# Values as weights in two attentions, X split beside a gate product, and query blocks in groups of two

## Chip, cores and metric

One core of a Trainium2 chip runs the whole program. The metric is the device time of one execution in microseconds (us). TensorE (PE) multiplies, VectorE (DVE) and ScalarE (ACT) work on its results, GpSimd (POOL) prepares weights, SyncE (SP) issues loads.

## What is computed

Three layers on 512 tokens of width 1024, in float32. The parts that matter here:

```python
def forgetting_attention(q, k, v, log_f):      # first layer, 8 heads of 64
    sc = q @ k.T * scale + (c[t] - c[s]),  causal
    return softmax(sc) @ v                     # then * silu(fg)
...
# second layer ends with
x = x + sigmoid(x @ ple_w_gate + ple_b_gate) * (p @ ple_w_proj)
...
def swa_sink_attention(x, pos, k_sh, v_sh, w_q, b_q, sinks, w_o, b_o):   # third layer, 16 query heads, 4 key heads
    scores = q @ kb * A_HEAD_DIM ** -0.5       # a block of 128 queries sees its own and the block before: 256 keys
    m = maximum(max(scores), sink); e = exp(scores - m)
    probs = e / (sum(e) + exp(sink - m))
    return (probs @ vb) @ w_o + b_o            # k_sh, v_sh = split(x @ kv_w + kv_b)
```

## The kernel before, in words

X lies with features on the partitions and the 512 tokens along the free dimension (8 tiles of 128x512). Every large product splits both factors into a high and a low part (fp32r) and sums three products per tile in a PSUM bank: high x high, high x low weights, low x high (lines 575 to 577). The weights stream in 238 blocks of 128x1024 through `W_raw`, and POOL splits them into `W_hi` and `W_lo`. Each engine has its own program, written by hand in the order in which it runs; semaphores join them. A table (`PHASES`, `PLAN`) lists the products, which engine reads their banks, and so which count a later tile waits for before it takes one of the four accumulation banks (`bank_free`). Some products are woven (`weave`): their first three tiles run together, feature tile by feature tile, while A is still being made.

The first attention (`softmax_attention(FOX, ...)`) has four pairs of heads and, for each, four query blocks (steps) with 128, 256, 384 and 512 keys. A step on TensorE: scores of both heads (each head in one half of the rows of the array), gates and mask added by bf16 products, transposes of the probabilities, and the weighing, where the transposed probabilities `PT` are the stationary operand and 64 columns of values move (line 772). A float32 matmul is two records in the trace, a transpose one. The output of a pair has tokens on the partitions, is scaled by the inverse sums (VectorE, line 1649), and turned back by four transposes (`turn_outputs`, line 719). The second attention (SWA) has eight pairs, four steps each, with 128 keys in the first and 256 in the others; both heads of a step go through one maximum (line 1616), four or two exponents on ACT (line 1183), transposes, a copy and the weighing. Two sets of score banks alternate by step (`score_bank`). The product of its values (`v3`) gives features on the partitions, and is turned by eight transposes.

In `embed(0)` ACT takes the sigmoid of each gate tile into `GATE`, VectorE multiplies by the projection and adds to X; when ACT has taken all eight, it splits X into `A_hi`, which the gate product itself still reads until then, and VectorE makes `A_lo` for the rotary product `rope3`, which is woven.

```python
                sums(f"gate{l}", into(lambda i: GATE[:, i, :], ACT.Sigmoid, f"ple_b{l}"))
                for i in range(KD):
                    if l == 0:
                        split(X[:, i, :], i, "ple0", embedded, i + 1)
```

## Time and profile before

| | us |
|---|---|
| median of three runs | 1557.76 (1557.06 to 1558.67) |
| the profiled execution | 1559.97 |
| its span, first to last instruction | 1556.9 |
| TensorE busy | 1529.2 |
| POOL, VectorE, ACT busy | 902.4, 715.6, 419.9 |

The span is what the trace shows; the profiled execution's own time includes 3.1 us outside it. TensorE's granted clock is full in every slice of the page. A busy TensorE is not TensorE at its peak, since records of matmuls overlap: the pace is read from start to start.

### The profile page before, as it was taken

How to read it: one execution, taken by the hardware profiler on the slowest of the kernel's cores; microseconds unless marked ns; L12 is line 12 of the kernel's file. 1: busy time of each engine (PE TensorE's matmuls, PEld its weight loads, DVE VectorE, ACT ScalarE, POOL GpSimd, SP SyncE). 2: the span in 40 equal slices, each digit the busy share in tenths (PEclk: the TensorE clock that was granted, in tenths of full speed). 3: DMA queues.
4: the chain of work that ended last, by engine and by line, in shares of the span. 5: the costliest groups of instructions: out<-in, count | busy, mean ns of one | idle time of the engine just before them, and what ended most of it. 6: DMA issues, size and time to landing. Idle time of an engine off the chain costs nothing.

```text
span 1556.9 us, 19863 instructions
## 1 busy us (share of the span) xinstructions
PE 1529.2 (98%) x7220; PEld 1239.3 (80%) x7220; DVE 715.6 (46%) x877; ACT 419.9 (27%) x845; POOL 902.4 (58%) x719
## 2 busy tenths in 40 slices
PE   9999999999999999999999999999999999999998
PEld 7777777788888788888888877867878888888876
DVE  5674566350026576103531255667667400552255
ACT  3223545133113332001210044655142200221031
POOL 7656023676631778666766655800549766776644
PEclk9999999999999999999999999999999999999999
DMA  6223011323320323333333322300213332222322
GB/s 208 95 82 95 15 41 35 101 81 95 95 68 20 114 75 115 95 95 95 94 99 104 95 68 81 122 15 1 83 53 122 100 102 95 95 95 95 98 78 81
DMA packets 36837, 132.30 MB, mean 85 GB/s; under 512 B 4105, under 2 KB 4385, under 8 KB 36770
## 3 DMA queue, kind: packets, MB, share of 16 engines
q1 hardware_dynamic: 35282, 128.16, 26.3%
q10 hardware_dynamic: 1488, 3.17, 0.6%
q8 instruction: 51, 0.84, 0.2%
q14 instruction: 16, 0.13, 0.0%
HBM read 129.20 MB, written 2.10 MB: 84 GB/s over the span
## 4 chain that ended last, share of the span: by engine, by line
PE 90%; DVE 4%; ACT 4%; DMA 1%; issue 1%; ACTq 0%; SPq 0%; DVEq 0%
PE PS L575 22%; PE PS L577 22%; PE PS L576 22%; PE PS L548 2%; PE PS L772 2%; PE PS L543 2%; PE PS L544 2%; PE PS L757 1%; PE PS L732 1%; PE PS L929 1%; DVE A_lo L1488 1%; PE PS L600 1%; PE PS L601 1%; PE PS L602 1%; PE PS L692 1%; PE PS L690 1%
## 5 line engine op out<-in xcount | busy, mean ns | idle before, releaser
L501 POOL TENSOR_TENSOR W_lo<-W_raw,W_hi 128x1024 fp32r<-128x1024 f32 x238 | 600.9, 2525 | 19.8
L498 POOL TENSOR_TENSOR HOLD<-HOLD 1x1 f32<-1x1 f32 x238 | 62.9, 264 | 616.4 <-PE PS L577 342.1
L575 PE MATMUL PS<-A_hi,W_hi 128*128 128x512 f32 x984 | 385.0, 391 | 0.0
L577 PE MATMUL PS<-A_lo,W_hi 128*128 128x512 f32 x984 | 382.9, 389 | 0.0
L576 PE MATMUL PS<-A_hi,W_lo 128*128 128x512 f32 x984 | 382.8, 389 | 0.0
L499 POOL TENSOR_SCALAR W_hi<-W_raw 128x1024 fp32r<-128x1024 f32 x238 | 247.2, 1039 | 0.0
L575 PEld LDWEIGHTS PS<-A_hi,W_hi 128*128 128x128 f32 x984 | 184.7, 188 | 39.7 <-issue 1.1
L576 PEld LDWEIGHTS PS<-A_hi,W_lo 128*128 128x128 f32 x984 | 184.7, 188 | 39.1 <-issue 1.0
L577 PEld LDWEIGHTS PS<-A_lo,W_hi 128*128 128x128 f32 x984 | 184.7, 188 | 38.7
L575 PE MATMUL PS<-H_hi,W_hi 128*128 128x512 f32 x512 | 199.2, 389 | 0.0
L576 PE MATMUL PS<-H_hi,W_lo 128*128 128x512 f32 x512 | 199.2, 389 | 0.0
L577 PE MATMUL PS<-H_lo,W_hi 128*128 128x512 f32 x512 | 199.2, 389 | 0.0
L1843 DVE TENSOR_TENSOR H_lo<-SQR,H_hi 128x512 f32 (+1 forms) x64 | 122.6, 1915 | 57.4 <-ACT H_hi L1383 57.4
L1380 ACT ACTIVATE RELU<-PS 128x512 f32<-128x512 f32 x64 | 38.0, 594 | 308.5 <-PE PS L577 300.7
L1841 DVE TENSOR_TENSOR SQR<-RELU 128x512 f32<-128x512 f32 x64 | 81.3, 1270 | 79.9 <-ACT RELU L1380 79.9
L576 PEld LDWEIGHTS PS<-H_hi,W_lo 128*128 128x128 f32 x512 | 96.1, 188 | 20.1
L577 PEld LDWEIGHTS PS<-H_lo,W_hi 128*128 128x128 f32 x512 | 96.1, 188 | 20.0
L575 PEld LDWEIGHTS PS<-H_hi,W_hi 128*128 128x128 f32 x512 | 96.1, 188 | 19.7
L1790 DVE TENSOR_TENSOR X<-X,PS 128x512 f32<-128x512 f32 x32 | 21.9, 687 | 177.9 <-PE PS L577 177.9
L1787 DVE SCALAR_TENSOR_TENSOR X<-X,PS 128x512 f32<-128x512 f32 x24 | 16.4, 687 | 173.4 <-PE PS L577 167.7
L1348 ACT ACTIVATE SQ<-X 128x512 f32<-128x512 f32 x28 | 17.8, 636 | 198.5 <-DVE X L1790 176.2
L543 PE MATMUL PS<-A_hi,W_hi 128*128 128x512 f32 x168 | 66.4, 396 | 2.1 <-ACT A_hi L1066 2.1
(293 smaller groups left out, 1978.6 us busy)
## 6 DMA issues: line engine op xcount, KB each, us to landing
W_raw<-in_weights SPq DMA_DIRECT2D x238, 512.0 KB, 3.5
X<-in_x SPq DMA_DIRECT2D x4, 512.0 KB, 6.3
out<-X ACTq DMA_DIRECT2D x8, 256.0 KB, 2.8
RELU<-in_ple_in ACTq DMA_DIRECT2D x2, 512.0 KB, 3.5
CONST<-in_constants SPq DMA_DIRECT2D x1, 849.5 KB, 10.1
PARAM<-in_params SPq DMA_DIRECT2D x1, 197.5 KB, 3.7
CONST<-in_constants SPq DMA_DIRECT2D x1, 192.0 KB, 8.6
NEG_C<-FF_PART ACTq DMA_DIRECT2D x3, 8.0 KB
```

What stands on the lines that cost most here:

```text
L498: pool.tensor_tensor(HOLD[:, 1 + s:2 + s], HOLD[:, 0:1], HOLD[:, 0:1], ALU.add)
L499: pool.tensor_scalar(W_hi[:, s, :], W_raw[:, r, :], 1.0, 1.0, ALU.mult, ALU.mult).then_inc(w_hi, 1)
L501: pool.tensor_tensor(W_lo[:, s, :], W_raw[:, r, :], W_hi[:, s, :].bitcast(F32), ALU.subtract).then_inc(w_lo, 1)
L543: pe.matmul(PS[:, i, :], W_hi[:, slot, w], hi[:, k, :], start=k == 0, stop=False)
L544: pe.matmul(PS[:, i, :], W_lo[:, slot, w], hi[:, k, :], start=False, stop=False)
L548: done = pe.matmul(PS[:, i, :], W_hi[:, slot, w], lo[:, k, :], start=False, stop=k == KD - 1)
L575: pe.matmul(PS[:, bank, :], W_hi[:, slot, w], hi[:, kk, :], start=first, stop=False)
L576: pe.matmul(PS[:, bank, :], W_lo[:, slot, w], hi[:, kk, :], start=False, stop=False)
L577: done = pe.matmul(PS[:, bank, :], W_hi[:, slot, w], lo[:, kk, :], start=False, stop=last)
L1380: act.activation(RELU[:, slot, :], bank, ACT.Relu).then_inc(by_act, 1)
L1841: dve.tensor_tensor(SQR[:, slot, :], RELU[:, slot, :], RELU[:, slot, :], ALU.mult).then_inc(h_sq, 1)
L1843: dve.tensor_tensor(H_lo[:, i, :], SQR[:, slot, :], H_hi[:, i, :].bitcast(F32), ALU.subtract).then_inc(h_lo, 1)
```

## The change

Both attentions now keep the values stationary: 64 columns of values per head are the weights and 128 columns of transposed probabilities move, one head into the upper, the other into the lower half of the output's partitions. The output so has features on the partitions, no transposes follow, and the inverse sums are spread over partitions by eight small products per pair (`spread_inverse`); VectorE multiplies the bank by them (`SHARE`). The second attention goes by groups of two query blocks: the two blocks of both heads share two score banks, with the mask put in first, and one maximum covers both blocks (1024 elements). Its values product has tokens stationary and 256 columns of weights moving, so the values need no turning, and the bias is now 256 columns of parameters. The first scores are issued ahead of that product, the second behind it. X after the gate product goes into buffers of its own (`B_hi`, `B_lo`): ACT splits tile i - 3 right behind the sigmoid of tile i, the gate is worked out in its PSUM bank, and the bank is freed by VectorE's addition instead of ACT.

```diff
-        ("down{0}b", 8, 2, "dve"), ("proj{0}b", 4, 0.25, "act"), ("gate{0}", 8, 1, "act")]
+        ("down{0}b", 8, 2, "dve"), ("proj{0}b", 4, 0.25, "act"), ("gate{0}", 8, 1, "dve")]
...
-PHASES += [("rope3", 10, 1, "act"), ("v3", 2, 1, "act"), ("out3", 8, 1, "dve")]
+PHASES += [("rope3", 10, 1, "act"), ("v3", 2, 1, "dve"), ("out3", 8, 1, "dve")]
...
-                ("head_g", 8), ("b_rope", 10), ("b_v", 2), ("sinks", Q_HEADS), ("b_o", 8),
+                ("head_g", 8), ("b_rope", 10), ("sinks", Q_HEADS), ("b_o", 8),
                 ("mix_g0", 8), ("mix_b0", 8), ("mlp_g0", 8), ("mlp_b0", 8), ("ple_b0", 8),
-                ("mix_g1", 8), ("mix_b1", 8), ("mlp_g1", 8), ("mlp_b1", 8), ("ple_b1", 8), ("w_pool", 2 * P)]
+                ("mix_g1", 8), ("mix_b1", 8), ("mlp_g1", 8), ("mlp_b1", 8), ("ple_b1", 8), ("w_pool", 2 * P), ("b_v", 2 * P)]
...
+            def window_values():
+
+                ph, banks = PLAN["v3"], VALUE_BANKS["v3"]
+
+                def multiply(b, t, k):
+                    slot, tokens = (ph.first + b) % W_SLOTS, slice(t * P, t * P + P)
+                    w = slice(k % 4 * 2 * P, (k % 4 + 1) * 2 * P)
+                    out = PS[:, banks[t // 2], t % 2 * 2 * P:(t % 2 + 1) * 2 * P]
+                    first, last = k == 0 and t % 2 == 0, k == KD - 1
+                    pe.matmul(out, B_hi[:, k, tokens], W_hi[:, slot, w], start=first, stop=False, skip_group_check=True)
+                    pe.matmul(out, B_hi[:, k, tokens], W_lo[:, slot, w], start=False, stop=False, skip_group_check=True)
+                    return pe.matmul(out, B_lo[:, k, tokens], W_hi[:, slot, w], start=False, stop=last,
+                                     skip_group_check=True)
+
+                pe.wait_ge(w_lo, ph.first + 1)
+                for t in range(NT):
+                    for k in range(4):
+                        done = multiply(0, t, k)
+                done.then_inc(block_done, 1)
...
+            def spread_inverse(S, p):
+
+                pe.wait_ge(S.inverted, p + 1)
+                if S is FOX and p == 0:
+                    pe.wait_ge(by_act, PLAN["late1"].before + 1)
+                for i in range(NT):
+                    for h in range(2):
+                        half, at = slice(h * HD, h * HD + HD), S.column(i, h)
+                        mm = pe.matmul(PS[half, SPREAD_BANK, i * P:i * P + P],
+                                       sum_columns(p)[:, at:at + 1].broadcast_to([P, HD]), const("ident"),
+                                       start=True, stop=True, skip_group_check=True)
+                mm.then_inc(S.spread, 1)
+
+            def weigh_step(S, v, values, moving):
+
+                p, i = v // NT, v % NT
+                keys_from, width = S.keys(i)
+                for j in range(width // P):
+                    for h in range(2):
+                        half = slice(h * HD, h * HD + HD)
+                        mm = pe.matmul(PS[half, O_BANK, i * P:i * P + P], values(p, keys_from // P + j)[:, half],
+                                       moving(h, j * P), start=j == 0, stop=(j + 1) * P == width, skip_group_check=True)
+                mm.then_inc(S.weighed, 1)
...
+                late_tile(0, SPREAD_BANK)
+                for v in range(FOX.steps):
+                    transposes(v, 0)
+                    transposes(v, 1)
+                    if v:
+                        if v % NT == 0:
+                            spread_inverse(FOX, v // NT - 1)
+                        weigh(v - 1)
+                    if v + 2 < FOX.steps:
                         scores(v + 2)
+                spread_inverse(FOX, FOX.pairs - 1)
+                weigh(FOX.steps - 1)
+                late_tile(1, 6)
...
+                    for h in range(2):
+                        pe.matmul(PS[:, score_bank(g, h), :], IDENT_B[:], WINDOW_B[:, 2 * c * P:2 * c * P + T], start=True,
+                                  stop=False, skip_group_check=True)
+                    for i in (2 * c, 2 * c + 1):
+                        first, width = swa_keys(i)
+                        for h in range(2):
+                            half = slice(h * HD, h * HD + HD)
+                            mm = pe.matmul(PS[:, score_bank(g, h), window_columns(i)], QK3[half, p + 2, i * P:i * P + P],
+                                           QK3[half, p // 4, first:first + width], start=False, stop=True,
+                                           skip_group_check=True)
+                    mm.then_inc(SWA.scored, 1)
...
+                scores(0)
+                window_values()
+                scores(1)
+                for g in range(2 * SWA.pairs):
+                    transposes(2 * g)
+                    transposes(2 * g + 1)
+                    if g:
+                        if g % 2 == 0:
+                            spread_inverse(SWA, g // 2 - 1)
+                        weigh(2 * g - 2)
+                        weigh(2 * g - 1)
+                    if g + 2 < 2 * SWA.pairs:
+                        scores(g + 2)
+                spread_inverse(SWA, SWA.pairs - 1)
+                weigh(SWA.steps - 2)
+                weigh(SWA.steps - 1)
...
-            from_a("rope3", "ple0", woven=True)
-            from_a("v3", "ple0", turn_values("v3", 2))
-            pe.wait_ge(roped, 10)
-            pe.wait_ge(v_ready, 4)
-            softmax_attention(SWA, (PR3, PT3, O_T3), lambda p: QK3[:, p + 2, :], lambda p: QK3[:, p // 4, :],
-                              lambda p, j: V3[:, j, p // 4, :], BAND_MASK_B, 3 * KD)
+            from_embedded("rope3", woven=True)
+            window_attention()
+            pe.wait_ge(SWA.shared, SWA.pairs)
...
+                for g in range(2 * SWA.pairs):
+                    p, c = g // 2, g % 2
+                    exponent(2 * g, 0)
+                    if g:
+                        copy(2 * g - 2)
+                    exponent(2 * g, 1)
+                    exponent(2 * g + 1, 0)
+                    exponent(2 * g + 1, 1)
+                    if c:
+                        act.wait_ge(SWA.sink_in, p + 1)
+                        act.activation(SMALL[:, 8:16], SMALL[:, 8:16], ACT.Exp).then_inc(SWA.sinked, 1)
+                        if p:
                             mixed(p - 1)
...
-                sums(f"gate{l}", into(lambda i: GATE[:, i, :], ACT.Sigmoid, f"ple_b{l}"))
+
+                def embedded_split(i):
+                    act.wait_ge(by_dve, PLAN["gate0"].before + i + 1)
+                    act.activation(B_hi[:, i, :], X[:, i, :], ACT.Copy).then_inc(a_hi, 1)
+
+                def gate(i, bank, at):
+                    act.activation(bank, bank, ACT.Sigmoid, bias=param(f"ple_b{l}", i)).then_inc(gate_open, 1)
+                    if l == 0 and i >= WOVEN:
+                        embedded_split(i - WOVEN)
+
+                sums(f"gate{l}", gate)
+                if l == 0:
+                    for i in range(KD - WOVEN, KD):
+                        embedded_split(i)
+                    return
...
+                def mix(p):
+                    dve.wait_ge(SWA.spread, p + 1)
+                    dve.tensor_copy(SHARE3[:], PS[:, SPREAD_BANK, :]).then_inc(SWA.shared, 1)
+                    dve.wait_ge(SWA.shared, p + 1)
+                    if p:
+                        dve.wait_ge(a_lo, stage_at + p)
+                    dve.wait_ge(SWA.weighed, NT * (p + 1))
+                    dve.tensor_tensor(MIX[:, 0, :], PS[:, O_BANK, :], SHARE3[:], ALU.mult).then_inc(mix_ready, 1)
+
+                maxima(0)
+                window_values(0)
+                window_values(1)
+                for g in range(2 * SWA.pairs):
+                    p, c = g // 2, g % 2
+                    if g:
+                        maxima(g)
+                    if c:
                         sinks(p)
-                    if before:
-                        copy(*before)
-                    before = next(((v, n, heads) for n, heads in S.groups(v) if n % 2), None)
-                    if i == 1 and p:
-                        outputs(p - 1)
-                    if i == 3 and p:
+                    if g:
+                        copy(2 * g - 1)
+                    if c == 0 and p:
+                        inverse(p - 1)
+                    if c and p:
                         mix(p - 1)
-                    if i == 0 and p >= 2 and not gate:
-                        low_part(p - 2, a_at, MIX[:, 0, :])
-                if before:
-                    copy(*before)
-                if not gate:
-                    low_part(S.pairs - 2, a_at, MIX[:, 0, :])
-                outputs(S.pairs - 1)
-                mix(S.pairs - 1)
-                if not gate:
-                    low_part(S.pairs - 1, a_at, MIX[:, 0, :])
+                    if c == 0 and p >= 2:
+                        low_part(p - 2, stage_at, MIX[:, 0, :])
...
+            def embedded_low(k):
+                dve.wait_ge(a_hi, KD * A_STAGE["ple0"] + k + 1)
+                dve.tensor_tensor(B_lo[:, k, :], X[:, k, :], B_hi[:, k, :].bitcast(F32), ALU.subtract).then_inc(a_lo, 1)
+
             def embed(l):
                 ph = PLAN[f"gate{l}"]
                 for i in range(KD):
-                    dve.wait_ge(by_act, ph.before + i + 1)
-                    dve.tensor_tensor(GATE[:, i, :], GATE[:, i, :], projection(i), ALU.mult).then_inc(gated, 1)
+                    bank = PS[:, i % ACC, :]
+                    dve.wait_ge(gate_open, KD * l + i + 1)
+                    dve.tensor_tensor(bank, bank, projection(i), ALU.mult).then_inc(gated, 1)
                     dve.wait_ge(gated, KD * l + i + 1)
-                    dve.tensor_tensor(X[:, i, :], X[:, i, :], GATE[:, i, :], ALU.add).then_inc(embedded, 1)
+                    dve.tensor_tensor(X[:, i, :], X[:, i, :], bank, ALU.add).then_inc(by_dve, 1)
                     if l == 0 and i:
-                        low_part(i - 1, KD * A_STAGE["ple0"], X[:, i - 1, :])
+                        embedded_low(i - 1)
```

TensorE in the middle of the second attention. PR are the probabilities and CONST the identity that turns them; L772 is the weighing, L732 scores, L739 mask, L719 the turning of an output. Before:

```order
L757 MATMUL PS<-CONST,PR 128x128 x4
L772 MATMUL PS<-V,PT 128x64 x4
L732 MATMUL PS<-QK 128x128 x2
L739 MATMUL PS<-BAND_MASK_B,IDENT_B 128x128 x2
L719 MATMUL PS<-CONST,O_T 128x128 x4
L757 MATMUL PS<-CONST,PR 128x128 x4
L772 MATMUL PS<-V,PT 128x64 x4
L732 MATMUL PS<-QK 128x256 x2
L739 MATMUL PS<-BAND_MASK_B,IDENT_B 128x256 x2
L757 MATMUL PS<-CONST,PR 128x128 x2
L772 MATMUL PS<-V,PT 128x64 x4
L732 MATMUL PS<-QK 128x256 x2
```

After, where L837 transposes, L729 spreads the inverse sums, L741 weighs, and L816 and L822 are mask and scores:

```order
L816 MATMUL PS<-WINDOW_B,IDENT_B 128x512 x2
L822 MATMUL PS<-QK 128x256 x4
L837 MATMUL PS<-CONST,PR 128x128 x6
L729 MATMUL PS<-CONST,SMALL 64x128 x8
L741 MATMUL PS<-PT,V 64x128 x8
L816 MATMUL PS<-WINDOW_B,IDENT_B 128x512 x2
L822 MATMUL PS<-QK 128x128 x2
L822 MATMUL PS<-QK 128x256 x2
L837 MATMUL PS<-CONST,PR 128x128 x8
L741 MATMUL PS<-PT,V 64x128 x6
```

Two steps of two transposes and weighings each became one group, in which all transposes stand together, the weighing is of the group before, and the turning is gone. ACT between the gate product and the rotary product (L1412 and L1415 before, L1498 and L1501 after). Before:

```order
L1367 ACTIVATE A_hi<-X,PARAM 128x512
L1368 ACTIVATE X<-X,PARAM 128x512
L1168 ACT_TABLE_LOAD
L1168 ACTIVATE GATE<-PS,PARAM 128x512 x8
L1066 ACTIVATE A_hi<-X 128x512 x8
L1412 ACTIVATE PS<-PS,PARAM 32x512 x4
L1415 ACTIVATE RAWQ<-PS,PARAM 128x512
```

After, with the sigmoid at L1480 and the split at L1477:

```order
L1480 ACT_TABLE_LOAD
L1480 ACTIVATE PS<-PS,PARAM 128x512 x4
L1477 ACTIVATE B_hi<-X 128x512
L1480 ACTIVATE PS<-PS,PARAM 128x512
L1477 ACTIVATE B_hi<-X 128x512
L1480 ACTIVATE PS<-PS,PARAM 128x512
L1477 ACTIVATE B_hi<-X 128x512
L1480 ACTIVATE PS<-PS,PARAM 128x512
L1477 ACTIVATE B_hi<-X 128x512
L1480 ACTIVATE PS<-PS,PARAM 128x512
L1477 ACTIVATE B_hi<-X 128x512 x4
L1498 ACTIVATE PS<-PS,PARAM 32x512 x4
```

Four of the eight splits, those of tiles 0 to 3, moved in among the sigmoids; the row with x4 at the end is the splits of tiles 4 to 7.

## Rows read from the trace of the kernel before

**Rows 1.** The page: busy time and share of TensorE.

```profile
PE 1529.2 (98%) x7220; PEld 1239.3 (80%) x7220; DVE 715.6 (46%) x877; ACT 419.9 (27%) x845; POOL 902.4 (58%) x719
```

**Rows 2.** Waits of TensorE in both attentions: total us, times, longest.

```profile
PE PS L757 <- ACT PR L1183: 4.3, 11, 0.8
...
PE PS L772 <- ACT PT L1192: 0.7, 1, 0.7
```

**Rows 3.** Stretches: length, then busy us and count of each engine, clock.

```profile
153.70:159.51 5.81, 5.03 (x31) 2.75 (x30) 1.75 (x4) 3.29 (x11) 3.53 (x3) 1.00 0.14 23
159.51:195.35 35.84, 35.61 (x286) 27.39 (x285) 20.88 (x44) 18.76 (x60) 0.00 (x0) 1.00 0.03 12
999.58:1090.59 91.01, 83.58 (x618) 64.63 (x616) 56.95 (x131) 47.72 (x168) 10.71 (x9) 1.00 0.08 24
1029.43:1038.72 9.29, 8.87 (x72) 6.87 (x71) 6.75 (x16) 5.26 (x21) 0.00 (x0) 1.00 0.00 1
```

**Rows 4.** TensorE in time order, second attention: start, length, instruction.

```profile
1032.14 0.70 PE L732 MATMUL PS<-QK 64*128 64x256 f32 x4
1032.77 0.39 PE L739 MATMUL PS<-BAND_MASK_B,IDENT_B 128*128 128x256 bf16 x2
1033.00 0.38 PE L757 MATMUL PS<-CONST,PR 128*128 128x128 f32 x2
1033.22 1.00 PE L772 MATMUL PS<-V,PT 128*128 128x64 f32 x8
1034.15 0.70 PE L732 MATMUL PS<-QK 64*128 64x256 f32 x4
```

**Rows 5.** TensorE in time order, stick-breaking attention.

```profile
225.63 0.39 PE L846 MATMUL PS<-SP_T,CONST 128*128 128x128 f32 x2
225.85 0.39 PE L843 MATMUL PS<-SP_T,CONST 128*128 128x128 f32 x2
...
234.05 0.39 PE L855 MATMUL PS<-ATT,V 128*64 128x128 f32 x4
234.37 0.70 PE L831 MATMUL PS<-SBQ,SBK 64*128 64x512 f32 x2
```

**Rows 6.** Time order, first attention, a step of 512 keys.

```profile
171.17 0.50 PE L757 MATMUL PS<-CONST,PR 128*128 128x128 f32 x3
...
171.37 1.23 DVE L1616 TENSOR_REDUCE SMALL<-PS 128x2 f32<-128x1024 f32 x1 [1.57 <-PE PS L739]
...
172.83 0.69 ACT L1183 ACTIVATE PR<-PS,SMALL 128x512 f32<-128x512 f32 x1 [0.64 <-DVE SMALL L1620]
...
173.51 0.68 ACT L1183 ACTIVATE PR<-PS,SMALL 128x512 f32<-128x512 f32 x1
```

**Rows 7.** Time order, second attention, ACT then TensorE.

```profile
1034.59 0.37 ACT L1192 ACTIVATE PT<-PS 128x256 f32<-128x256 f32 x1
1034.85 0.47 ACT L1183 ACTIVATE PR<-PS,SMALL 128x256 f32<-128x256 f32 x1
...
1035.47 0.66 PE L757 MATMUL PS<-CONST,PR 128*128 128x128 f32 x4 [0.29 <-ACT PR L1183]
```

**Rows 8.** Stretch of the second attention's values product.

```profile
999.58:1010.46 10.88, 10.88 (x50) 8.96 (x49) 2.29 (x3) 5.44 (x8) 7.18 (x6) 1.00 0.36 101
```

**Rows 9.** TensorE, two records of 256 columns, matrix memory.

```profile
449.14 0.59 PE L929 MATMUL PS<-V,DEC 128*128 128x256 f32 x2
```

**Rows 10.** Time order, from the gate product to the rotary product.

```profile
942.28 0.69 ACT L1168 ACTIVATE GATE<-PS,PARAM 128x512 f32<-128x512 f32 x1 [4.75 <-PE PS L577]
...
943.54 0.50 PE L543 MATMUL PS<-A_hi,W_hi 128*128 128x512 f32 x1 [1.29 <-ACT A_hi L1066]
...
948.40 0.98 PE L548 MATMUL PS<-A_lo,W_hi 128*128 128x512 f32 x3 [1.17 <-DVE A_lo L1488]
```

**Rows 11.** Transfers of the start; stretch from 8 to 10 us, GB/s last.

```profile
PARAM<-in_params SPq DMA_DIRECT2D x1, 197.5 KB, 3.7
...
8.00:10.00 2.00, 1.81 (x6) 0.78 (x5) 2.00 (x4) 2.00 (x5) 0.03 (x1) 1.00 1.02 379
```

More of the change, by code:

```diff
@@ L731, in scores @@
                         half = slice(h * HD, h * HD + HD)
[L732 to L734 removed]
+                        pe.matmul(PS[:, score_bank(v, h), 0:width], QK[half, p, i * P:i * P + P],
+                                  QK[half, p + 4, 0:width], start=True, stop=False)
                     for h in range(2):
@@ L760, in weigh @@
-                def weigh(v, n, heads):
-                    p, i = v // NT, v % NT
-                    keys_from, width = S.keys(i)
-                    read(n)
-                    if n % S.per_pair == 0 and p >= 2:
-                        pe.wait_ge(mix_ready, mixed_before + p - 1)
-                    if S is FOX and n == S.per_pair:
-                        pe.wait_ge(by_act, PLAN["late1"].before + 1)
-                    for h in heads:
-                        half = slice(h * HD, h * HD + HD)
-                        for j in range(width // P):
-                            at = S.at(v, h) + j * P
-                            mm = pe.matmul(PS[:, p % 2, i * P + h * HD:i * P + h * HD + HD], PT_[:, n % 2, at:at + P],
-                                           values(p, keys_from // P + j)[:, half], start=j == 0, stop=(j + 1) * P == width)
-                    mm.then_inc(S.weighed, 1)
@@ L1219, in stick_breaking @@
+                copy(SWA.steps - 2)
+                mixed(SWA.pairs - 1)
             def stick_breaking():
```

420 lines of the change are left out of this document (225 added, 195 removed).

## Prediction

> **What bounds the kernel now.** I read the page first: TensorE is busy for 1529.2 of the 1556.9 us of the span [rows 1], so time can only come from less work on TensorE or from its few waits. Two stretches are touched. In the list of waits, the stretch of the second attention (values product included) holds 4.3 us of idle before the transposes of the probabilities, waiting for exponents on ACT [rows 2]. The table by stretch gives lengths: three pairs of heads of the first attention take 35.84 us (11.95 each) with TensorE busy in 35.61; the second attention from the values product to the output product takes 91.01 us, busy in 83.58; one of its pairs takes 9.29 us [rows 3]. So the first attention is bound by TensorE's own work, and the second by work plus a wait in each pair.
>
> For prices I read starts, not durations, because records overlap. In the second attention a step of 256 keys is: scores 0.63 us, masks 0.23, two transposes 0.22 (0.11 each), eight records of the weighing 0.93 [rows 4]. A matmul of the weighing is two records, each with 128x128 probabilities as weights and 64 columns moving; they come about every 0.11 us, no faster than transposes with 128 columns, so the columns saved by moving only 64 are lost to loading weights.
>
> **Part 1: values as weights.** The trace already has this form: stick-breaking multiplies with 64-column weights, one head into each half of the output partitions. There, four records of 128 columns (both heads, two each) start at 234.05, and work in another shape starts at 234.37; with unpaired 128x128 weights two records of 128 columns take 0.22 (225.63 to 225.85) [rows 5]. Of the 0.32 I give 0.22 to the four, two heads for the price of one, and 0.1 to the change of the array's shape. A key block of both heads now costs four records of 0.112 = 0.45 us; it will cost 0.22. Bounds: 0.22 (the unpaired two) and 0.45 (no gain); the row allows 0.32 at most. I take 0.22, since it is the same form and the change of shape must have its share.
>
> What it adds: eight matmuls per pair that spread the inverse sums over the partitions. In the same form they are four paired sets, 4 x 0.22 = 0.88 us. What it removes: four transposes of the output, 0.44 us. Also, each block of weighing is now in another shape of the array than its neighbours. Leaving a shape costs the 0.1 above, and a score block carries 0.3 in all (0.63 for 0.43 of columns at 0.107 per 128 and record pair, and of the weighing's 0.93 before it some 0.09 [rows 4]). I price the weighing block's entry at 0.15 (from 0.1 to 0.3, the score block's total).
>
> The Trainium skill says in TensorEngine Tiling (Array Packing), Key Properties, that changing the tiling mode drains TensorE, which speaks against this change. The row shows less than a full drain: the four records end at 234.44 (234.05 plus 0.39), and the next shape has started at 234.37 [rows 5]. By the row the 16 switches more than before cost 1.6 us; by a full drain, 0.17 each, 2.7.
>
> First attention, per pair: transposes 20 x 0.11 = 2.2; weighing 10 x 0.22 = 2.2 (before 40 x 0.112 = 4.48); scores 2.13, gates and masks 1.54, both unchanged; spread 0.88; switches 4 x 0.455 = 1.82 (before 4 x 0.3). Sum 10.77, where the same sum for before gives 11.99 against 11.95 measured. But a wait appears. In the step of 512 keys the maximum takes 1.23 us (from 171.37), the first exponent starts at 172.83 and the second at 173.51 [rows 6], so the transposes of the second head can start 3.16 us after the scores' end (171.17 [rows 6]), and they used to be later than that because weighing filled the time. Now there are only transposes 0.66, weighing 0.59 and the next scores 0.74 = 1.99 in between; the first head's transposes end at 2.94, and the block ends at 3.6 instead of 2.87. That is 0.73 per pair: 11.5 against 11.95. Three pairs save 1.35; the head of the loop (to the end of the fourth scores, 5.81 us now [rows 3]) loses its 0.7 wait for the copy [rows 2] and two small weighings and saves 1.55; at the end the inverse now sits in front of the last weighing, +0.7; the last pair's transposes go, -0.5. **First attention -2.7 us** (0 to -5).
>
> **Part 2: groups of two query blocks.** TensorE per pair then: transposes 1.54, weighing 7 x 0.22 = 1.54 (was 3.14), spread 0.88, masks 4 x 0.22 = 0.88, score columns 1.5, switches 2 x 0.555; sum 7.45. Score banks are still two sets, so a group's scores wait for the exponents of the group two before, which closes a loop: scores to maximum 0.2; maximum over 1024 elements 1.23 [rows 6]; negation and handover 0.23; four exponents with a copy between them 2.29 (exponents of 0.47 each, a copy of 256 columns puts the next off by 0.26 and one of 512 by about twice that, 0.62 from the last start to the released transposes [rows 7]); then on TensorE four transposes 0.5, entry 0.15, spread 0.88, four key blocks 0.88, switch 0.1, masks 0.44, switch 0.2, scores 0.64 = 3.8. Together 7.75 us for two groups, that is for one pair, against 9.29 now. VectorE needs about 6.8 per pair (two maxima 2.5, five passes of 0.61 to 0.72, small ones 0.9), so it is hidden under 7.75 by less than 1 us. What is late next is this loop, by way of the exponents, before each even group.
>
> From the end of the rotary product (999.58): first scores 1.4; values product 11.6; second scores 1.5; from there until the third pair's maximum 11.2 (reaching 25.7); five pairs of 7.75; tail 10.9. Sum 75.3 against 91.0: **-15.7 us**. The values product is 96 matmuls of 256 columns in place of 48 of 512, 0.227 us each now [rows 8]. No row has 256 columns in this type. Bounds: 0.11 (a mask matmul of 256 columns, or a transpose with its weights [rows 4]) and 0.43 (the two-record type at 256 columns, 0.59 less 0.38 = 0.21 per record [rows 9]). I take 0.12, half a 512 plus a little. Its transposes, copies and waits go, as first scores and exponents now lie beside it; that cover is 11.6 us against about 5 of rotary work left and 5 of maxima and exponents.
>
> **Part 3: X split beside the gate product.** Now the rotary product starts 1.46 us late (943.54 instead of 942.08) and waits again until 948.40, 1.3 us; together 2.8 [rows 10]. The new buffer lets four tiles be split early, but the banks are now free only after VectorE's addition. The third woven tile needs bank 2, so the addition of gate tile 6, and on VectorE the low part of tile 4 stands before it, whose split on ACT stands behind the sigmoid of tile 7: 942.28 + 0.58 sigmoid, 0.65 split, 0.61 low part, 0.72 product, 0.7 addition = 945.5, while TensorE has four matmuls until 943.0. It waits 2.6. **-0.2 us** (+1 to -2.8).
>
> **Part 4, beside the description.** The value bias becomes 256 columns of parameters, 127 KB more in front of X at the start. TensorE waits for X there, and transfers run at 379 GB/s [rows 11]: **+0.35 us**.
>
> Sum: -2.7 -15.7 -0.2 +0.35 = -18.2. The profiled execution took 1559.97 us (3.1 outside its span), the median of runs 1557.76; from the median: **1539.5 us**.
>
> **Rivals.**
> - *VectorE and ACT set the pace of a group.* The wider maximum releases four exponents at once, later than two small ones would; copies stand behind it on VectorE. For it: less than 1 us of slack per pair. Against it: busy sum 6.8. The Trainium skill's TensorEngine Tiling, PSUM Bottleneck, says that tiling speeds up TensorE and not the reading of PSUM, which may become the bottleneck; the trace agrees in that 6.8 is near 7.75. With 8.5 to 9.3 per pair the time is 1546 to 1550. Chance 0.17.
> - *The 256-column matmuls take 0.21, as a record of the other type does*: +9.1, 1548.6. Chance 0.08; at 0.43 it would be +30, 1569, chance 0.02.
> - *The waits vanish* (transposes start on each first exponent): pairs of 7.6 and no stall of 0.73: 1536.3. Chance 0.08.
> - *Slower:* 128 columns are too short for two heads side by side, because records are paced by their weights (0.112 each, as in the weighing of before [rows 4]): key block 0.45, spread 1.8. That adds 12.8 less 2.2 of stall in the first attention, 1.8 x 8 in the second: about +25, 1565. It decides above about 0.38 per key block. Against it is the paired set [rows 5]. Chance 0.03.
> That parts 1 and 2 change nothing is excluded by a TensorE that is busy for 98% of the span: what is taken from it there has no other cover.
>
> **Numbers.** Forecast 0.62 (1537 to 1544). The range takes in the two likely rivals above and the vanished waits below: 1535 to 1549.5. A measurement here can tell 0.2%, 3 us; only the last rivals are slower: faster 0.94, same 0.01, slower 0.05.
>
> **What would show it.** Right: weighing records in pairs a few ns apart, 0.22 per key block; pairs of the second attention at 7.6 to 7.9; one wait before the fourth step's transposes of the first attention, near 0.5 to 0.8; the third woven tile waiting for VectorE near 2.6. Wrong: an even group's maximum starting over 0.3 after its scores end (VectorE binds), or the values product lasting 15 us or more.

## The result

Before and after were timed in turns, four runs each: 1558.22 us before (1557.06 to 1561.31) and 1541.41 us after (1538.26 to 1543.81). The ratio is 0.9893, 95% interval 0.988 to 0.9906: 16.8 us faster, where 18.2 were forecast. The profiled execution of the changed kernel is the slowest of its four runs, 1543.81 us, and its mean granted clock is the lowest (0.996; 0.997, 0.997 and 0.999 in the others). That matters below.

The page of the changed kernel, which answers to [rows 1]:

```profile
PE 1516.2 (98%) x7372; PEld 1220.4 (79%) x7372; DVE 699.2 (45%) x847; ACT 415.8 (27%) x843; POOL 898.9 (58%) x719
PEclk9999999999999999999999999999999999999999
```

A 9 in the clock's row stands for 90% or more of a slice of 39 us, so this row cannot show a fall of the clock of 3 us, here or before: the kernel before has two such falls in its trace, although its row is full too. TensorE is still the bound and has 13 us less to do. Its waits, as in [rows 2] (total, times, longest), those of the touched stretches only:

```profile
PE PS L540 <- DVE X L2001: 2.4, 1, 2.4
PE PS L837 <- ACT PR L1267: 2.1, 3, 1.6
PE PS L775 <- ACT PR L1238: 2.0, 4, 1.1
```

The first is new, between gate and rotary product. The second is in the second attention, once 1.6 us, at its start. The third is the stall that was forecast in the first attention. The stretches, in the columns of [rows 3]: three pairs of the first attention, the second attention up to the output product, its values product, one pair of it, and three short pieces that are spoken of below. The last three numbers of a row are the granted clock, the share of the DMA engines and GB/s.

```profile
158.90:193.58 34.68, 33.98 (x328) 22.28 (x329) 21.47 (x46) 18.93 (x62) 0.00 (x0) 1.00 0.06 17
999.50:1076.89 77.39, 75.02 (x722) 54.65 (x721) 53.51 (x99) 44.69 (x166) 10.72 (x9) 0.98 0.09 28
1000.89:1012.51 11.62, 11.62 (x99) 11.57 (x97) 4.28 (x6) 5.29 (x14) 6.03 (x5) 1.00 0.24 62
1045.21:1052.92 7.71, 7.71 (x79) 5.28 (x78) 6.27 (x13) 5.09 (x21) 0.00 (x0) 1.00 0.00 0
941.84:944.29 2.45, 0.00 (x1) 0.00 (x1) 2.05 (x4) 0.88 (x3) 2.37 (x2) 1.00 0.50 189
944.29:947.70 3.41, 3.41 (x9) 2.66 (x10) 3.28 (x4) 1.24 (x2) 0.83 (x1) 0.53 0.38 98
1019.60:1023.10 3.50, 3.50 (x22) 1.99 (x18) 0.81 (x3) 1.29 (x7) 0.00 (x0) 0.51 0.01 5
```

| part | forecast, us | trace of the profiled runs, us |
|---|---|---|
| start | +0.35 | +0.46 |
| first attention, to the stick-breaking scores | -2.7 | -2.34 (146.44 to 207.36 before, 146.91 to 205.49 after) |
| between the attentions (norm statistics) | 0 | +0.6 |
| gate to rotary product | -0.2 | +1.2 |
| second attention | -15.7 | -13.6 (91.01 before, 77.39 after) |
| the second embedding | 0 | -1.6 |
| sum | -18.2 | -15.3 (spans 1556.9 and 1541.6) |

A pair of the first attention takes 11.56 us (forecast 11.5), one of the second 7.71 (7.75), the values product 11.62 (11.6), 0.12 per matmul. The last two rows of the fence above show what the sum had not: right behind two waits of TensorE the granted clock is 0.53 and 0.51 for some 3.4 us, so nearly all of it at the lower level, 1.2 GHz. The kernel before has that behind the norm at 532.7 and behind the norm of the second embedding at 1140.3; the changed one behind the norm at 531.5, at 944.5 and at 1019.6, but not in the second embedding (every trace has one more in its last 4 us). That is the -1.6 in the table, and no gain of the change.

### The profile page after: what moved, and what is told of

Its sections match the earlier page's. It is cut to its first block, busy times and chain, and to the rows that moved or that the text cites. A ratio compares the mean times of both kernels' runs of the same rounds, so it can differ in the third digit from the quotient of the medians.

```text
span 1541.6 us, 20139 instructions
## 1 busy us (share of the span) xinstructions
PE 1516.2 (98%) x7372; PEld 1220.4 (79%) x7372; DVE 699.2 (45%) x847; ACT 415.8 (27%) x843; POOL 898.9 (58%) x719
## 4 chain that ended last, share of the span: by engine, by line
PE 91%; DVE 4%; ACT 3%; issue 1%; DMA 0%; ACTq 0%; SPq 0%; DVEq 0%
PE PS L572 22%; PE PS L573 22%; PE PS L574 22%; PE PS L545 2%; PE PS L540 2%; PE PS L541 2%; PE PS L994 1%; PE PS L741 1%; PE PS L822 1%; DVE A_lo L1573 1%; PE PS L598 1%; PE PS L599 1%; PE PS L597 1%; PE PS L837 1%; PE PS L702 1%; PE PS L729 1%
## 5 line engine op out<-in xcount | busy, mean ns | idle before, releaser
L572 PE MATMUL PS<-A_hi,W_hi 128*128 128x512 f32 x912 | 357.0, 391 | 0.0
L574 PE MATMUL PS<-A_lo,W_hi 128*128 128x512 f32 x912 | 354.9, 389 | 0.0
L573 PE MATMUL PS<-A_hi,W_lo 128*128 128x512 f32 x912 | 354.8, 389 | 0.0
L572 PEld LDWEIGHTS PS<-A_hi,W_hi 128*128 128x128 f32 x912 | 171.2, 188 | 37.5 <-issue 1.1
L573 PEld LDWEIGHTS PS<-A_hi,W_lo 128*128 128x128 f32 x912 | 171.2, 188 | 36.3 <-issue 1.0
L574 PEld LDWEIGHTS PS<-A_lo,W_hi 128*128 128x128 f32 x912 | 171.2, 188 | 35.5
L540 PE MATMUL PS<-A_hi,W_hi 128*128 128x512 f32 x144 | 56.9, 395 | 0.8 <-ACT A_hi L1129 0.8
```

Source lines behind the costliest of these rows:

```text
L540: pe.matmul(PS[:, i, :], W_hi[:, slot, w], hi[:, k, :], start=k == 0, stop=False)
L572: pe.matmul(PS[:, bank, :], W_hi[:, slot, w], hi[:, kk, :], start=first, stop=False)
L573: pe.matmul(PS[:, bank, :], W_lo[:, slot, w], hi[:, kk, :], start=False, stop=False)
L574: done = pe.matmul(PS[:, bank, :], W_hi[:, slot, w], lo[:, kk, :], start=False, stop=last)
```

## The experiments

All start from the changed kernel, and diffs are against it. Ratios are to the kernel before, run in turns on the same chip.

### X split at once

```diff
-                    if l == 0 and i >= WOVEN:
-                        embedded_split(i - WOVEN)
+                    if l == 0 and i:
+                        embedded_split(i - 1)
...
-                    for i in range(KD - WOVEN, KD):
-                        embedded_split(i)
+                    embedded_split(KD - 1)
```

> ACT splits tile i - 1 of X, not tile i - 3, behind the sigmoid of gate tile i; nothing else is changed. My theory: the 2.45 us wait of the third woven tile and the slow matmuls behind it (the granted clock was at half from 944.3 to 947.7) come from VectorE, which stood before the low part of tile 4 until ACT had split it behind the last sigmoid. Then the wait goes and the clock does not fall there: matmuls that started at 948.50 start near 944.2, 4.3 us earlier, and the median goes from 1541.4 to about 1537. Rival A: the clock falls at its own times; then only the wait goes, 2.4 us, and half speed shows up nearby. Rival B: the low parts on VectorE are late anyway, and the wait only moves to the next low part: under 1 us.

Measured: 1537.21 us (1535.69 to 1538.84), ratio 0.9862 (0.9846 to 0.9879); the changed kernel was 1541.41. First what the changed kernel did there, in order of time:

```profile
941.45 0.39 PE L541 MATMUL PS<-B_hi,W_lo 128*128 128x512 f32 x1
941.56 1.14 ACT L1477 ACTIVATE B_hi<-X 128x512 fp32r<-128x512 f32 x2
942.21 0.69 DVE L1992 TENSOR_TENSOR B_lo<-X,B_hi 128x512 fp32r<-128x512 f32 x1 [2.63 <-ACT B_hi L1477]
942.82 0.69 DVE L1999 TENSOR_TENSOR PS<-PS,PROJ_B 128x512 f32<-128x512 f32 x1
943.55 0.69 DVE L2001 TENSOR_TENSOR X<-X,PS 128x512 f32<-128x512 f32 x1
944.29 0.62 PE L540 MATMUL PS<-B_hi,W_hi 128*128 128x512 f32 x1 [2.45 <-DVE X L2001]
944.71 0.63 PE L541 MATMUL PS<-B_hi,W_lo 128*128 128x512 f32 x1
...
948.50 0.84 PE L545 MATMUL PS<-B_lo,W_hi 128*128 128x512 f32 x3
```

VectorE had nothing to do for 2.63 us, because its low part of tile 4 stood ahead of work whose inputs were ready. Three of its operations later TensorE's bank came free, and the next matmuls came 0.42 us apart, not 0.23. The same place with the split at once:

```profile
942.18 0.39 PE L541 MATMUL PS<-B_hi,W_lo 128*128 128x512 f32 x1
942.41 0.39 PE L540 MATMUL PS<-B_hi,W_hi 128*128 128x512 f32 x1
942.63 0.39 PE L541 MATMUL PS<-B_hi,W_lo 128*128 128x512 f32 x1
942.86 0.84 PE L545 MATMUL PS<-B_lo,W_hi 128*128 128x512 f32 x3
...
944.90 0.84 PE L545 MATMUL PS<-B_lo,W_hi 128*128 128x512 f32 x3
```

No wait and no fall of the clock here. The product's first matmul starts at 940.77 in the changed kernel and at 941.50 in this one; the three of the last row come 7.73 us behind it there and 3.40 here, 4.3 less, and my theory holds for this place. The heads-apart kernel below has the changed kernel's code here and the same wait of 2.45 us, but in its trace the clock did not fall behind it:

```profile
940.91 0.39 PE L540 MATMUL PS<-B_hi,W_hi 128*128 128x512 f32 x1
...
947.06 0.84 PE L545 MATMUL PS<-B_lo,W_hi 128*128 128x512 f32 x3
```

There the three matmuls come 6.15 us behind the first. So of the 4.3 us some 2.75 are the wait, with the gaps around it, and 1.58 the clock. Rival A is right in part, since this run has falls of its own elsewhere, one at the start and one behind the norm at 891 (first row of the stretches):

```profile
891.10:894.50 3.40, 3.40 (x13) 3.01 (x14) 2.69 (x5) 0.00 (x0) 0.00 (x0) 0.52 0.30 118
...
996.13:1071.73 75.60, 72.20 (x713) 53.72 (x719) 53.49 (x99) 44.70 (x166) 10.72 (x9) 1.00 0.09 28
```

The second row gives the second attention with the clock held: 75.60 us, where 75.3 was forecast. (Its count of matmuls, 713 against 722 in the changed kernel, is lower because some records are missing; so busy times of TensorE can't be compared to 0.2 us between traces, and starts can.) The medians are 4.2 us apart, but at the same mean clock the runs of the two kernels are 2.5 to 2.8 apart (0.999: 1535.69 and 1535.78 against 1538.26; 0.997: 1538.64 against 1541.41): the wait itself is certain, the fall behind it a matter of the run.

### Scores between the halves of the values product

```diff
                 done.then_inc(block_done, 1)
+                between()
                 pe.wait_ge(w_lo, ph.first + 2)
...
-                window_values()
-                scores(1)
+                window_values(lambda: scores(1))
                 for g in range(2 * SWA.pairs):
                     transposes(2 * g)
+                    if g == 0:
+                        scores(2)
                     transposes(2 * g + 1)
...
-                    if g + 2 < 2 * SWA.pairs:
+                    if 0 < g < 2 * SWA.pairs - 2:
                         scores(g + 2)
...
                 maxima(0)
+                maxima(1)
                 window_values(0)
...
-                    if g:
+                    if g > 1:
                         maxima(g)
```

> The second group's scores stand between the two halves of the values product, the third group's behind the first two transposes, and VectorE takes the second maximum ahead of the values. My theory: the 1.6 us wait before the second group's transposes (its maximum and exponents have only 3.7 us of other work beside them) and the half clock that follows it (1020 to 1023) cost about 3 us together, and both go: from the window scores to the output product about 74.3 us in place of 77.4, the time 1538.3. Rival A: the clock falls elsewhere, only 1.6 goes. Rival B: the first exponents then wait for the copy on ACT behind the first transposes, and the wait comes back one group later: no gain.

Measured: 1541.33 us (1538.89 to 1541.59), ratio 0.9892 (0.9875 to 0.9908), no gain in the median. The profiled run, its fastest, shows the stretch as expected, 74.43 us, 1.17 less than the 75.60 of the experiment before, both at full clock, with 0.7 us of waits left (0.4 and 0.3). Below it stands the fall behind the 2.45 us wait of part 3, which this kernel still has:

```profile
997.51:1071.94 74.43, 72.30 (x711) 53.74 (x718) 53.94 (x99) 45.03 (x166) 10.72 (x9) 1.00 0.09 29
943.14:946.55 3.41, 3.41 (x10) 2.69 (x9) 3.28 (x8) 0.63 (x1) 0.00 (x0) 0.53 0.53 154
```

The other three runs have mean clocks of 0.995, 0.996 and 0.996, at or below the lowest of the changed kernel (0.996). They have no traces, so that falls of the clock ate the gain there is argued from the clock alone.

### The value bias loaded later

```diff
-            sp.dma_start(PARAM[:], params).then_inc(p_in, 16)
+            sp.dma_start(PARAM[:, 0:PARAM_AT["b_v"][0]], params[:, 0:PARAM_AT["b_v"][0]]).then_inc(p_in, 16)
...
+            sp.dma_start(PARAM[:, PARAM_AT["b_v"][0]:], params[:, PARAM_AT["b_v"][0]:]).then_inc(bias_in, 16)
...
+                    dve.wait_ge(bias_in, 16)
                     dve.wait_ge(v3_summed, 1)
```

> The value bias (the last 256 columns of the parameters) is loaded last at the start, behind the constants. My theory: 127 KB ahead of X cost 0.46 us; the 32 columns' matmuls of the first product at 12.09 start at 11.63 as before the change, and everything behind 0.4 us earlier. Rival: the order of transfers around the parameters shifts by itself and the start is 0.46 late still. The single time cannot tell 0.4 us; the stretch to the second product in the trace can.

Measured: 1541.27 us in one run. The first scores of the first attention start at 146.46, against 146.91 in the changed kernel and 146.44 before it. But kernels with the bias ahead of X start them at 146.27 to 146.89 in the other experiments (heads apart 146.27, scores first 146.46, scores between 146.65, weighing first 146.89; two more at 148.2 and 148.4, behind a fall of the clock and a wait), and the two later kernels with the bias behind at 146.94 and 146.45. The start varies by 0.6 us by itself, so my theory is not shown, and the term of +0.35 is lost in that.

### Heads apart

```diff
-                for j in range(width // P):
-                    for h in range(2):
+                for h in range(2):
+                    for j in range(width // P):
```

> In the weighing of both attentions all key blocks of the first head are issued before those of the second, so neighbouring matmuls no longer stand in different halves of the output. The same matmuls otherwise. My theory: two heads run side by side only because they alternate; apart, a key block costs 0.43 in place of 0.21: 8.8 us more in the first attention less about 2 of its waits, 12 in the second, 1560. Rival: a 64-column stationary is simply loaded in half the time, whichever half it goes to; then the time stays at 1541.

Measured: 1542.82 us in one run. A pair of the first attention grew from 11.56 to 12.32 us, one of the second from 7.71 to 7.76; the whole first attention took 61.34 us against 58.58, and the second 76.03 against the 75.60 with the clock held. That is 3.2 us more. The time alone shows less, since this trace has one fall of the clock before its end and the changed kernel's three. My theory had 2.2 us more in a pair of the first, less some 0.5, and 1.5 in one of the second; the rival had nothing. Both failed. The weighing of four key blocks (16 records) and what follows, in this kernel:

```profile
177.26 1.53 PE L741 MATMUL PS<-PT,V 128*64 128x128 f32 x16
178.72 0.59 PE L757 MATMUL PS<-QK 64*128 64x384 f32 x2
```

The same in the changed kernel:

```profile
176.86 1.04 PE L741 MATMUL PS<-PT,V 128*64 128x128 f32 x16
177.83 0.59 PE L757 MATMUL PS<-QK 64*128 64x384 f32 x2
```

And the first four records of it alone, all of one head, again with the heads apart:

```profile
177.26 0.60 PE L741 MATMUL PS<-PT,V 128*64 128x128 f32 x4
```

Four records of one head last 0.60 us, where four of two heads last 0.39 [rows 5]: three steps of 0.11 ahead of the last record in place of one. So a record with a weight of 64 columns costs as much alone, 0.11, as one with 128 [rows 5], the rival falls, and the halves do run side by side. But the whole block takes 1.46 us to the next scores, not 0.97 + 0.87 = 1.84: from the sixth start on (177.70) a second row of records, 0.11 apart like the first, runs between those of the first. The trace names no head, but the first row ends with its eighth record at 178.02 and the second with its eighth at 178.51, so I read it as the second head, which stands behind the first in the program. Three key blocks lose 0.27 (a pair: 0.27 + 0.49), and the blocks of one and two of the other steps next to nothing.

### Weighing first in the step of 512 keys

```diff
                 for v in range(FOX.steps):
+                    if v % NT == 3:
+                        weigh(v - 1)
                     transposes(v, 0)
                     transposes(v, 1)
-                    if v:
+                    if v and v % NT != 3:
```

> First attention, step of 512 keys alone: the weighing of the step before (three key blocks, 0.8 us) is issued ahead of this step's transposes instead of behind them. Nothing else is changed. My theory: the wait before those transposes (0.55 at 172.03, of 2.0 in all four pairs) is time in which TensorE had this work at hand; it goes, and a pair takes 11.05 in place of 11.56, the first attention 2 us less. Rival: the weighing waits as long for the second head's copy, which stands behind the wide maximum on VectorE (it ends at 172.2); then a pair stays at 11.4 to 11.6.

Measured: 1539.48 us in one run, pairs of 11.08 us in place of 11.56. The step in the changed kernel:

```profile
172.03 0.22 PE L762 MATMUL PS<-FOX_MASK_B,IDENT_B 128*128 128x128 bf16 x1
172.58 1.32 PE L775 MATMUL PS<-CONST,PR 128*128 128x128 f32 x8 [0.33 <-ACT PR L1238]
```

And with the weighing first:

```profile
183.12 0.22 PE L762 MATMUL PS<-FOX_MASK_B,IDENT_B 128*128 128x128 bf16 x1
183.42 0.88 PE L741 MATMUL PS<-PT,V 128*64 128x128 f32 x12
184.22 1.09 PE L775 MATMUL PS<-CONST,PR 128*128 128x128 f32 x8
```

For the pair my theory holds: the time from the last mask to the next start shrinks from 0.55 to 0.3 us, and the transposes of both heads then follow without a gap (1.09 in place of 1.32). For the whole it fails. The first attention was to take 2 us less and takes 57.96 against 58.58, only 0.6 less:

```profile
146.89:204.85 57.96, 55.22 (x476) 38.39 (x481) 31.41 (x60) 27.34 (x85) 6.77 (x5) 1.00 0.08 27
```

From the first step of 512 keys to the second it still takes 11.59, so only two pairs gain, 0.48 each, and in the last pair the wait of 1.1 turns into two of 0.83 (the copy, the rival's wait, since no scores stand ahead of it there) and 0.89 (the inverse). The single time is 1.9 us under the changed kernel's median; 0.6 of that is shown to be the edit's.

### Scores first, and a copy taken twice

Scores first: in the loop of the second attention `scores(g + 2)` stands ahead of `spread_inverse` and `weigh`, otherwise the same lines. Copy twice:

```diff
+                    own(dve.tensor_copy(SHARE3[:], PS[:, SPREAD_BANK, :]))
+                    own.wait()
                     dve.tensor_copy(SHARE3[:], PS[:, SPREAD_BANK, :]).then_inc(SWA.shared, 1)
```

> Second attention: a later group's scores are issued behind the transposes, ahead of the weighing, in place of behind it. My theory: the pair of 7.71 us is TensorE's own work (7.58) with one wait of 0.13, and the loop through the score banks, although it comes out at 7.75 in my sum, has only that much to give; so a pair takes 7.5 to 7.7. Rival: the loop sets the pace; it loses 2 us per pair by this, and a pair falls to what VectorE needs, 6.8 to 7.2.

> Second attention: VectorE copies the spread inverse sums twice, 0.68 us more per pair; nothing else is changed. My theory: VectorE is busy for 6.27 of 7.71 us per pair and nobody waits for its copies, so a pair stays within 0.1 of 7.71. Rival (VectorE sets the pace): a pair grows by 0.3 to 0.7, 8.0 to 8.4.

Scores first: 1544.46 us in one run, pairs of 8.30 us, slower, which neither theory had. VectorE shows why (1047.0 to 1047.8 are the scores whose maximum stands in the last row):

```profile
1048.99 0.69 DVE L1795 COPY SHARE<-PS 128x512 f32<-128x512 f32 x1 [1.63 <-PE PS L729]
1049.96 0.69 DVE L1800 TENSOR_TENSOR MIX<-PS,SHARE 128x512 f32<-128x512 f32 x1 [0.28 <-PE PS L741]
1050.57 1.21 DVE L1767 TENSOR_REDUCE SMALL<-PS 128x4 f32<-128x1024 f32 x1
```

The maximum is ready to run from 1047.9 and starts 2.7 us later, behind the multiplication that waits for the weighing, which now comes after the scores. The edit took one wait and made another, so it says nothing of what the loop alone would give; a version with VectorE's order turned as well was not tried.

Copy twice: 1543.98 us in one run, against 1543.81 in the profiled run without it; pairs of 7.71 and 7.72 us with VectorE busy for 6.97:

```profile
1048.84:1056.56 7.72, 7.56 (x78) 5.28 (x78) 6.97 (x14) 5.16 (x22) 0.00 (x0) 1.00 0.01 2
```

VectorE's amount of work does not set the pace of a pair; the place of one operation in its order can. Only at the end of the attention does TensorE wait for the copy, in front of the output product:

```profile
1077.06 0.50 PE L572 MATMUL PS<-A_hi,W_hi 128*128 128x512 f32 x1 [0.65 <-DVE SHARE L1797]
```

### All four edits, and the late tile

X split at once, bias later, scores between and weighing first in one kernel:

> Four edits together: X split at once, the bias loaded later, scores between the halves of the values product, weighing first in the step of 512 keys. By the stretches at full clock they give 2.45 (the wait in front of the third woven tile), 0.4, 1.1 (the second attention took 75.5 against 76.6 where the clock held) and 2, together 6 us, and two of the waits after which the clock fell are gone, 1.7 us each where it would have fallen: 1534 median, from 1533 to 1536. Rival: the clock falls after other waits instead; then 1535 to 1537.

Measured: 1535.35 us (1534.16 to 1536.03), ratio 0.9849 (0.9836 to 0.9863), inside the expected 1533 to 1536. (The 75.5 and 76.6 in the expectation are the 74.43 and 75.60 above, read to a microsecond later.) That it lies inside is in part luck: two terms of the expectation did not come, the bias (0.4, not shown) and most of the weighing (0.6 for 2), and how much of the rest is the clock can't be told from medians. The profiled run has no fall of the clock until its last 4 us. At the end of the first attention it has two waits left:

```profile
194.53 0.88 PE L744 MATMUL PS<-PT,V 128*64 128x128 f32 x12 [0.83 <-DVE PT L1730]
195.34 1.09 PE L778 MATMUL PS<-CONST,PR 128*128 128x128 f32 x8
197.33 0.87 PE L732 MATMUL PS<-CONST,SMALL 128*64 128x128 f32 x12 [0.89 <-DVE SMALL L1734]
```

From the last 512-column scores to the first stick-breaking scores it takes 14.22 us, TensorE busy in 12.34:

```profile
190.68:204.90 14.22, 12.34 (x99) 9.29 (x98) 4.80 (x10) 3.77 (x10) 0.00 (x0) 1.00 0.00 1
```

The last kernel puts half of the late value tile, which stood behind all this, into the first gap:

```diff
+                    if v == FOX.steps - 1:
+                        late_tile(1, 2, range(0, 4))
                     if v % NT == 3:
                         weigh(v - 1)
...
-                late_tile(1, 6)
+                late_tile(1, 2, range(4, KD))
...
-                copy(FOX.steps - 1)
                 inverse(FOX.pairs - 1)
+                copy(FOX.steps - 1)
```

> The four edits of the run before, and at the end of the first attention half of the late value tile (2.7 us of products) ahead of the last step's weighing and transposes, the other half behind the last weighing; the last inverse on VectorE ahead of the last copy; the tile's bank is one of the score banks. My theory: TensorE waits there for 0.83 us (a copy) and 0.89 us (the inverse), and both are covered; of them about 0.4 comes back in front of the stick-breaking scores, which now wait until ACT has read the tile's bank. From the last 512-column scores at 190.7 to the first stick-breaking scores 12.9 us in place of 14.2, and the median 1534. Rival: the copies and the inverse are late by the same amounts wherever the tile stands, since ACT and VectorE follow the transposes; then the stretch stays within 0.3 of 14.2.

Measured: 1532.78 us (1531.71 to 1535.06), ratio 0.9833 (0.9818 to 0.9848). The intervals of the last two kernels overlap, but the trace tells them apart. The same stretch:

```profile
190.19:203.77 13.58, 13.18 (x105) 9.73 (x103) 5.26 (x11) 4.37 (x11) 0.76 (x2) 1.00 0.00 0
```

The stretch is 0.64 us shorter, less than the 1.3 expected; both old waits are gone from the list, and one of 0.4 stands before the scores, as expected. Four transposes of 0.45 us that used to follow the scores now stand ahead of them and inside this stretch, which makes it 1.1 by the same work. The profiled runs are 2.2 us apart and the medians 2.6, so at least half of either is not shown to come from this edit. Against the kernel before, this version is 1.67% faster, the changed kernel 1.07%.

## Why the forecast came out as it did

**First attention, -2.7 forecast, -2.34 measured: right, for the reason given.** Key blocks cost 0.22, the pair has the new wait before the step of 512 keys, and it takes 11.56. Three pairs gave 1.16 of the 1.35 forecast, the head of the loop 1.08 of 1.55, and the end, where 0.2 more was forecast, 0.1 less. The heads-apart run shows that two heads do share the time, for which the forecast had one row. What my "slower" rival describes, records paced by their weights, is what one head alone does.

**Second attention, -15.7 forecast: right at full clock.** With the clock held the stretch is 75.60, so -15.4; 1.8 us of the profiled run's 77.39 are the clock at the lower level at 1019.6 to 1023. Each term stood: product 11.62, pair 7.71. In the changed kernel's row TensorE is busy for all of a pair's 7.71; the 7.56 of the row of copy twice lacks the record of one mask matmul. By the starts there is one short wait in a pair: from the second transpose to the third it takes 0.235 us (1046.445 to 1046.680), where transposes beside it come 0.11 apart. So TensorE's own work is some 7.58 and the wait 0.13, where I had 7.45 of work and a loop of 7.75: the two are so close that the sum could not tell which binds, and scores first did not settle it. VectorE, the rival with 0.17, was not it: it is busy for 6.27 (6.8 forecast), and 0.68 more left the pair as it was. Entry into the weighing costs 0.15 and leaving it 0.1, as taken; the Trainium skill (TensorEngine Tiling (Array Packing), Key Properties) says that changing the tiling mode drains TensorE. The trace shows a cost at these places, but 0.25 per block is below the 2 x 0.17 that a full drain would be by the prediction's estimate from [rows 5].

**Gate to rotary product, -0.2 forecast, +1.2 measured: the term that was wrong.** The start came 1.47 us earlier, the old wait of 1.3 went, the new wait was 2.45 (2.6 forecast). What is missing in the sum is the clock: 3.4 us at the lower level behind the wait, 1.6 us. The heads-apart trace has this code and no fall here, and so gives the term with the clock held:

```profile
940.91:998.29 57.38, 54.87 (x242) 44.90 (x241) 36.84 (x38) 32.44 (x51) 39.14 (x30) 1.00 0.31 94
```

From the rotary product's first matmul to the first window scores that is 57.38 us, against 58.73 in the changed kernel and 57.50 before (942.08, where the gate product ends, to 999.58): -0.1, where -0.2 was forecast. The wait and the gain were right, and the clock is nearly the whole miss. I had costed a wait at its own length. And I had taken VectorE's order as given, where the wait was one of order: splitting at once removed it.

**The rest.** The +0.6 between the attentions is one VectorE operation of the norm (128x4 elements) that took 1.33 us, 0.16 in the kernel before; in the other nine kernels with the change it took 0.22 to 1.02. In all ten a 16 KB transfer of the queue for instructions starts within 0.5 us of it (at 529.10 here, the operation at 528.81), and in the kernel before none does within 14 us. That the operation waits for its program is a guess from this; no run tests it. The parameters' +0.35 can't be told from nothing.

The sum was off by 2.9 in the profiled run: 0.1 at the start, 0.35 in the first attention, 0.6 in the norm, 1.4 behind the gate and 2.1 in the second attention (3.4 of these two together are falls of the clock), less 1.6 for a fall that only the kernel before had. With the clock held the terms measured add up to 0.46 - 2.34 + 0.6 - 0.1 - 15.4 = -16.8. The medians give 16.8 too, inside the range; that the two agree so well is in part luck, since runs of both kernels hold falls of the clock.

Two sums of the rivals are off by their own figures, and neither changes the forecast: 96 matmuls at 0.21 in place of 0.12 are 8.6 us, not 9.1, and a key block of 0.45 with a spread of 1.8 makes a pair of the second attention 10.0, so 2.2 more, not 1.8.

## What to carry to other kernels

When work leaves TensorE, ask what the engines behind it have queued in front of the operation that frees its next bank: of the 4.3 us that the split at once saved at its place, some 2.7 were an engine waiting in order for something that was not needed yet, and 1.6 the clock behind that. Price a wait of TensorE by its length and by what its clock may do behind it, and when two kernels differ by 1 to 3 us, compare the clocks of their runs and the stretches of their traces at full clock, not two medians. Work that stands behind a gap (a weighing, half a product) can be moved into it, but look for the operation on the other engine that waits for the moved one.

## What the hardware showed beside this

**The clock after waits.** Of the ten traces with the change, seven have the 2.45 us wait at 942, and behind it the granted clock fell in six; in the three without it there was no fall at that place. Behind the 1.6 us wait of the second attention it fell in four of the seven that have it. Not every fall has a wait ahead of it: the two of the kernel before, one at 891.2 (split at once) and one at 1483.2 (heads apart) come behind a norm in which TensorE has no gap over 0.11 us, but 16 records of one moving column each, started over 1.6 us. Each fall lasts about 3.4 us and costs some 1.6 us, and which waits are hit differs from run to run: the changed kernel's four runs go from 1538.26 us at a mean clock of 0.999 to 1543.81 at 0.996.

**A slow operation at a fixed place.** In all ten the second group's negation on VectorE (128x4 elements) took 0.95 to 0.98 us, and 0.16 in all other groups:

```profile
1015.49 0.97 DVE L1770 SCALAR_TENSOR_TENSOR SMALL<-SMALL,NEG_SINK 128x4 f32<-128x4 f32 x1
1016.49 0.47 ACT L1267 ACTIVATE PR<-PS,SMALL 128x256 f32<-128x256 f32 x1 [8.72 <-DVE SMALL L1770]
1017.84 0.55 PE L837 MATMUL PS<-CONST,PR 128*128 128x128 f32 x3 [1.57 <-ACT PR L1267]
```

It makes half of the 1.57 us wait; with the scores between, it took 0.95 as well, at 1007.50, but beside the values product. No transfer of the queue for instructions lies within 1.5 us of it in seven of the ten, so what was found at the norm does not explain it. What VectorE does in that time is open.

**Records out of order.** As the spacing in the heads-apart run shows (two rows of records, each 0.11 apart, from the sixth start on), matmuls of one half of the output started before earlier ones of the other half; the trace does not name them. It would explain why the order of heads cost 1.46 us per four key blocks and not 1.84.
